# Split-half products for the attention values of every second chunk

## What is computed

```python
z = einsum('bqhd,bkhd->bhqk', q, k) * SB_SCALE + bias
mask = kpos[None, :] < qpos[:, None]
log_rest = where(mask, log_sigmoid(-z), 0.0)
after = cumsum(log_rest, axis=3, reverse=True) - log_rest
a = where(mask, exp(log_sigmoid(z) + after), 0.0)
out = einsum('bhqk,bkhd->bqhd', a, v)
```

## Time and profile before

| | |
|---|---|
| median of three runs | 1857.78 us |
| the profiled execution | 1855.77 us, its span 1854.0 us |
| granted TensorE clock, mean | 0.999 |
| busy over the span | PE 98%, PEld 93%, DVE 47%, ACT 28%, POOL 14% |
| the four pairs | about 68 us to 425 us of the span |
| one pair's 24 chunks | from 70.2 us; the next k projection starts at 139.98 us |

### The profile page before, as it was taken

One profiled execution on the slowest core, in us unless ns is written; L12 is line 12 of the kernel. 1 busy time (PEld: TensorE's weight loads), 2 busy tenths in 40 slices (PEclk: granted clock), 3 DMA queues, 4 the chain that ended last, 5 costly groups with the idle time before them and its releaser, 6 DMA issues.

```text
span 1854.0 us, 28837 instructions
## 1 busy us (share of the span) xinstructions
PE 1809.1 (98%) x11113; PEld 1721.2 (93%) x11113; DVE 871.3 (47%) x1111; ACT 524.3 (28%) x838; POOL 263.5 (14%) x309
## 2 busy tenths in 40 slices
PE   6999999999999999999999999999999999999997
PEld 6878787879799899999999889999999999999996
DVE  5565657475334423232242575552145542455536
ACT  5575757481100100000022542221112210122224
POOL 1121212120133211111111000000100001000002
PEclk9999999999999999999999999999999999999999
DMA  5202020205411111111131131111111111111312
GB/s 168 69 24 68 23 68 23 68 13 180 131 46 40 36 49 51 57 34 40 51 137 58 35 122 49 45 45 46 45 46 45 44 50 42 51 51 44 131 30 97
DMA packets 162282, 113.73 MB, mean 61 GB/s; under 512 B 5389, under 2 KB 152213, under 8 KB 161947
## 3 DMA queue, kind: packets, MB, share of 16 engines
q1 hardware_dynamic: 161035, 108.34, 19.6%
q10 hardware_dynamic: 1200, 4.75, 0.7%
HBM read 95.86 MB, written 13.40 MB: 59 GB/s over the span
## 4 chain that ended last, share of the span: by engine, by line
PE 87%; ACT 5%; DVE 4%; issue 2%; DMA 0%; SPq 0%; DVEq 0%; ACTq 0%; POOL 0%; POOLq 0%
PE ps L1490 67%; PE ps L1500 9%; PE misc L1584 2%; ACT zl L739 1%; ACT zl L744 1%; PE misc L1476 1%; PE ps L1770 1%; PE ps L1828 1%; PE ps L1714 1%; PE ps L1568 1%; PE misc L1788 1%; PE ps L1476 1%; ACT zl L749 1%; PE ps L1569 1%; PE ps L1574 0%
## 5 line engine op out<-in xcount | busy, mean ns | idle before, releaser
L1490 PE MATMUL ps<-h_hi,w_lo 128*128 128x344 f32 x1896 | 404.4, 322 | 1.9 <-DVE up L1359 1.1
L1490 PE MATMUL ps<-h_lo,w_hi 128*128 128x344 f32 x1896 | 402.8, 321 | 0.0
L1490 PE MATMUL ps<-h_hi,w_hi 128*128 128x344 f32 x1896 | 400.7, 320 | 0.0
L1072 DVE TENSOR_TENSOR w_lo<-stage,w_hi 128x1024 fp32r<-128x1024 f32 x148 | 198.6, 1342 | 335.8 <-POOL w_hi L573 334.8
L573 POOL TENSOR_SCALAR w_hi<-stage 128x1024 fp32r<-128x1024 f32 x148 | 158.8, 1073 | 1301.5 <-PE ps L1490 1064.7
L1490 PEld LDWEIGHTS ps<-h_hi,w_lo 128*128 128x128 f32 x1896 | 319.5, 188 | 4.3 <-issue 1.4
L1490 PEld LDWEIGHTS ps<-h_lo,w_hi 128*128 128x128 f32 x1896 | 321.2, 189 | 0.0
L1490 PEld LDWEIGHTS ps<-h_hi,w_hi 128*128 128x128 f32 x1896 | 316.3, 188 | 0.0
L1500 PE MATMUL ps<-h_hi,w_lo 128*128 128x344 f32 x408 | 135.6, 332 | 0.6 <-DVE a_raw L1167 0.5
L1359 DVE TENSOR_TENSOR up<-ps,work 128x1032 f32<-128x1032 f32 x44 | 54.2, 1233 | 166.6 <-PE ps L1490 163.3
L1500 PE MATMUL ps<-h_lo,w_hi 128*128 128x344 f32 x408 | 130.9, 321 | 0.0
(11 more groups left out here) (273 smaller groups left out, 2545.7 us busy)
## 6 DMA issues: line engine op xcount, KB each, us to landing
stage<-in_w_in SPq DMA_DIRECT2D x48, 512.0 KB, 3.9
stage<-in_w_up SPq DMA_DIRECT2D x44, 512.0 KB, 3.7
stage<-in_w_down SPq DMA_DIRECT2D x16, 448.0 KB, 3.3
stage<-in_w_branch SPq DMA_DIRECT2D x24, 256.0 KB, 2.7
x_scratch<-trunk SPq DMA_DIRECT2D x1, 4128.0 KB, 12.3
x_back<-x_scratch SPq DMA_DIRECT2D x1, 4128.0 KB, 13.5
x_tok<-in_x_prompt SPq DMA_DIRECT2D x8, 512.0 KB, 8.0
kv_pg<-in_cache_k SPq DMA_DIRECT2D x16, 256.0 KB, 3.8
```

The costliest lines, as they stand in the source:

```text
L1072: V.tensor_tensor(w_lo[par][:, :, :], stage[par][:, :, :], w_hi[par][:, :, :].bitcast(F32), ALU.subtract).then_inc(w_lo_made, 1)
L1490: last = M(ps[par][:, c, :], w[par][:, k, :], x[:, c * CH:(c + 1) * CH], start=(k == 0 and s == 0), stop=(k == n - 1 and s == 2))
```

## The change

- In even chunks `values` stays as it is. In odd chunks it is three fp32r products: `v_lo` with `att_hi`, `v_hi` with `att_lo`, `v_hi` with `att_hi`.
- Once a pair POOL makes `v_hi` (1024 columns, after `v_tok`), and DVE at its step 1 makes `v_lo` (1024 columns).
- For each odd chunk k POOL makes `att_hi` (behind `s_hi(k + 2)` in its queue; there is one buffer, so it also waits for the values of chunk k - 2), and DVE makes `att_lo` in place of `att` at the end of its step k + 3. For chunks 21 and 23 this lies behind the last `s_lo` and ahead of the last `w_lo`.
- There are three `att` buffers, not four, and `k_f` and `v_f` now lie under `att_hi`, `att2` and `v_hi`.
- PE takes the values at even steps c: first those of chunk c - 4, then those of chunk c - 5, with one increment of `pv_done` behind both. Before, it took c - 5 and c - 4 at odd steps.

```diff
-        att = [sb(f"att{i}", [P, HALF], F32, s_att) for i in range(2)] + [k_f[:, 0:HALF], k_f[:, HALF:2 * HALF]]
+        att = [sb(f"att{i}", [P, HALF], F32, s_att) for i in range(2)] + [att2]
...
+                def att_hi_of(c):
+
+                    W = CHUNKS[c][3]
+                    pool.wait_ge(att_ready, p * NCK + (c + 1))
+                    pool.wait_ge(pv_done, p * NCK + (c - 1 + NATT))
+                    pool.sem_inc(hi_begun, 1)
+                    nc.gpsimd.tensor_scalar(att_hi[:, 0:W], att[c % NATT][:, 0:W], 1.0, 0.0,
+                                            ALU.mult, ALU.add).then_inc(ahi_made, 1)
+
+                pool.wait_ge(vtok_made, p + 1)
+                pool.sem_inc(hi_begun, 1)
+                nc.gpsimd.tensor_scalar(v_hi, v_tok[:, :, :], 1.0, 0.0, ALU.mult, ALU.add).then_inc(vh_made, 1)
...
+                    if c >= 3 and c % 2 == 1:
+                        att_hi_of(c - 2)
+                att_hi_of(NCK - 1)
...
+                def att_lo_of(c):
+
+                    W = CHUNKS[c][3]
+                    dve.wait_ge(ahi_made, p * (NCK // 2) + (c + 1) // 2)
+                    a = att[c % NATT][:, 0:W]
+                    V.tensor_tensor(att_lo[c % NATT][:, 0:W], a, att_hi[:, 0:W].bitcast(F32), ALU.subtract).then_inc(alo_made, 1)
...
+                    if c == 1:
+                        dve.wait_ge(stack_in, p * 64 + 64)
+                        dve.wait_ge(vh_made, p + 1)
+                        V.tensor_tensor(v_lo, v_tok[:, :, :], v_hi.bitcast(F32), ALU.subtract)
+                    if c >= 4 and c % 2 == 0:
+                        att_lo_of(c - 3)
                 sums_lo(NCK - 1)
+                att_lo_of(NCK - 3)
+                att_lo_of(NCK - 1)
                 split_lo(1, p * 4 + 5)
...
-                    pe.wait_ge(att_ready, p * NCK + (c + 1))
-                    M(misc[:, q0:q0 + W], v_tok[:, kb, :], att[c % NATT][:, 0:W], start=top, stop=last,
-                      skip_group_check=True).then_inc(pv_done, 1)
+                    out = misc[:, q0:q0 + W]
+                    if c % 2 == 0:
+                        pe.wait_ge(att_ready, p * NCK + (c + 1))
+                        t = M(out, v_tok[:, kb, :], att[c % NATT][:, 0:W], start=top, stop=last, skip_group_check=True)
+                    else:
+                        pe.wait_ge(alo_made, p * (NCK // 2) + (c + 1) // 2)
+                        lo = att_lo[c % NATT][:, 0:W]
+                        M(out, v_lo[:, kb, :], att_hi[:, 0:W], start=top, stop=False, skip_group_check=True)
+                        M(out, v_hi[:, kb, :], lo, start=False, stop=False, skip_group_check=True)
+                        t = M(out, v_hi[:, kb, :], att_hi[:, 0:W], start=False, stop=last, skip_group_check=True)
+                    return t
...
-                    if c % 2 == 1 and 0 <= c - LAG_VALUES - 1 < NCK:
-                        values(c - LAG_VALUES - 1)
-                        values(c - LAG_VALUES)
+                    if c % 2 == 0 and c >= LAG_VALUES:
+                        done = 0
+                        for chunk in (c - LAG_VALUES, c - LAG_VALUES - 1):
+                            if 0 <= chunk < NCK:
+                                pv, done = values(chunk), done + 1
+                        pv.then_inc(pv_done, done)
```

More of the change, by code:

```diff
@@ L198, in build @@
         s_pair.close()
+        s_split = ExitStack()
+        sb("keys_below", [P, 3 * T], F32, s_split)
+        v_lo_all = sb("v_lo", [P, T], F32R, s_split)
+        att2 = sb("att2", [P, HALF], F32, s_split)
+        att_hi = sb("att_hi", [P, T - HALF], F32R, s_split)
+        v_hi_all = sb("v_hi", [P, T], F32R, s_split)
+        v_hi, v_lo = (v[:, 0:TP].rearrange("p (a b) -> p a b", b=P) for v in (v_hi_all, v_lo_all))
+        s_split.close()
+        s_low = ExitStack()
+        sb("split_below", [P, 4 * T], F32, s_low)
+        att_lo2 = sb("att_lo2", [P, HALF], F32R, s_low)
+        s_low.close()
         s_dec = ExitStack()
@@ L233, in build @@
         s_att.close()
+        s_low = ExitStack()
+        sb("att_below", [P, 14 * HALF], F32, s_low)
+        att_lo = [sb(f"att_lo{i}", [P, HALF], F32R, s_low) for i in range(2)] + [att_lo2]
+        s_low.close()
         spat = sb("spat", [P, SG, T], F32, s_mix)
@@ L326, in build @@
         (
-            params_in, gpre_in, consts, par_ps, par_sb, ss_made, std_made, rs_made, xn_made, xt_ps,
+            vh_made, ahi_made, alo_made, params_in, gpre_in, consts, par_ps, par_sb, ss_made, std_made, rs_made, xn_made, xt_ps,
             h_hi_made, w_hi_made, w_lo_made, unit_done, biasp_made, q_hi_made, kf_made, k_hi_made,
@@ L341, in build @@
         ) = (sem(n) for n in (
-            "params_in", "gpre_in", "consts", "par_ps", "par_sb", "ss_made", "std_made", "rs_made",
+            "vh_made", "ahi_made", "alo_made", "params_in", "gpre_in", "consts", "par_ps", "par_sb", "ss_made", "std_made", "rs_made",
             "xn_made", "xt_ps", "h_hi_made", "w_hi_made", "w_lo_made", "unit_done", "biasp_made",
```

## The result

The changed kernel takes 1869.36 us (median of 6 runs, 1868.17 to 1870.52), the one before, beside it, 1858.39 (6 runs, 1853.86 to 1860.72). The ratio is 1.0063, with a 95% interval of 1.0053 to 1.0073: 11.0 us slower, 9.8 to 13.6. The prediction was 1866.2 in a range of 1853 to 1875. Its sign and mechanism hold; the size is the top end of what it gave for its likeliest case (+8.4, 5 to 11). Of its three chances the largest (0.55) had gone to "the same", and 0.63% lies just past that bound, in the 0.39.

A forecast was written before the change was run, and what follows sets the result against it. Within a pair ACT bounds wide chunks, PE the narrow stretches and the tail. Three terms gave 1.25 to 2.7 us a pair, taken as 2.1: +8.4 on 1855.77 is 1864.2, as a median 1866.2 (range 1853 to 1875).

The forecast's parts named there:

- its likeliest case: The prediction's own forecast: four pairs add 8.4 us (5 to 11), 1862 to 1871; chance 50%.
- the same: Outcome not told from no change, about 0.5% or 9.3 us: between 1848.5 and 1867.1; chance 0.55.
- the 0.39: Chance of slower, above 1867.1: 0.24 from the forecast's own case and 0.15 from DVE's lag feeding back.
- The bound: In a pair, ACT where chunks are wide; cheaper matmuls count where ACT waits for PE (1.40, 1.15 us) and in the tail.
- First narrow stretch: Around chunks 8 to 11: ACT's wait for chunk 10 comes back one chunk later, plus 0.8 to 1.8 us a pair.
- Second narrow stretch: Chunks 20 to 23: same order, PE's chain from weights 16 reaches 123.1 against 122.89; plus 0.15 to 0.6 us a pair.
- The tail: End of a pair: values 20 ahead of the q projection start it 0.75 us later, what follows is shorter; net 0.3.
- The cover of the last `w_lo`: End of a pair: `w_lo` done at 139.6, PE needs it at 140.7, so 1.1 us of cover are left.
- The sum: Per pair 1.25 to 2.7 us, taken as 2.1 by half of the port waits; four pairs +8.4 us (5 to 11).
- DVE's lag feeds back all along: Rival: port waits make wide steps DVE's, plus 4 to 5 us per pair, 16 to 20 in all, 1876; chance 15%.
- The lag is absorbed: Rival: port waits near none, only the new order costs, 0.3 to 0.6 us per pair, 1856 to 1861; chance 25%.
- Faster: Rival: ACT's waits for PE go and don't come back, at most 2.55 us per pair, 1848, likelier 1852; chance 10%.

The follow-up runs named there:

- e11: The changed kernel without `att_hi`, `att_lo` and `v_lo`: new order and three fp32r products, `v_hi` kept; 1864.43 us, ratio 1.0038.
- e10: The changed kernel without `att_hi` and `att_lo`; `v_hi`, `v_lo`, the order and three fp32r products stay; 1865.63 us, ratio 1.0044.
- e2: The changed kernel without `att_lo`, the second product taking `att_hi` in its place; 1867.82 us, ratio 1.0058.
- e1: The kernel before with the new order of values (even steps, chunk c - 4 first), all native products, no halves; 1866.61 us, ratio 1.0052.
- the ladder: Pair periods: before 95.02; order alone 98.08; with fp32r products 96.85; with `v_lo` 97.35; with `att_hi` 97.75; with `att_lo` 98.19 us.
- e4: The kernel before with the values of one chunk (c - 5) at every step, all native; 1858.37 us, ratio 1.0007.
- e8: The kernel before with the two values of an odd step moved behind the scores of the next step, all native; 1858.34 us, ratio 1.0006.
- e6: The kernel before with values at even steps but the older chunk (c - 5) still first, all native; 1862.12 us, ratio 1.0024.
- e5: The kernel before's order (odd steps, c - 5 then c - 4) with halves made for even chunks, odd ones native; 1865.68 us, ratio 1.0049.
- e7: The changed kernel with the two values of an even step moved behind the next step's scores; 1880.24 us, ratio 1.0124.
- e12: As e7, with the last `w_lo` of a pair put ahead of `att_lo(21)` and `att_lo(23)` on DVE; 1876.63 us, ratio 1.0107.

## Why the prediction was right, and where its terms were off

Three of the signs that it gave for itself did not come: `s_lo(7)` was later than its 0.3 to 1.3 us, a pair took 3.17 longer and not 1.3 to 2.7, and PE's busy time did not fall. The two waits of ACT, the clock in the pairs and the three products 0.24 apart came as said.

**The bound.** It said that extra time counts in the narrow stretches, where ACT waits for PE, and in the tail. The wide steps, from chunk 11 to chunk 20, took 0.13 us less than before, the two narrow stretches 2.90 more, the tail 0.43. Right.

**First narrow stretch (0.8 to 1.8 forecast, 1.4 in the sum).** It took 1.87 in the second pair, and 2.31 in the first (97.85 - 69.42 against 94.35 - 68.23). The mechanism was right, waits vanished before chunk 10 and came back before 11. Its lower bound, with no lateness of DVE, was 0.8; e11, which has next to none, shows 26.90 - 26.03 = 0.87. Its chain from the end of `s_lo(7)` to chunk 11 was summed to 3.74 and took 97.85 - 93.87 = 3.98. What was under-sized is the lateness: `s_lo(7)` came 1.54 later, forecast 0.3 to 1.3. POOL's instructions held `sums` and `att_lo` too, which had been left out of the sum: `sums` beside `v_hi` took 0.80, and its group's mean rose from 346 ns before to 373 with `v_hi` alone (e10), 394 with `att_hi` (e2) and 416 in the changed kernel. The Trainium skill (GPSIMD Engine Reference, section 8, Key points) says that GpSimd contends with VectorE's instructions of two SBUF inputs; these rows agree, for `sums` as well.

**Second narrow stretch (0.15 to 0.6 forecast, took 1.03).** This is the term that failed most. Without lateness (e11) it is already (56.03 - 26.90) - (54.60 - 26.03) = 0.56 from chunk 11 to 23, and 0.69 from chunk 20 on ((56.03 - 48.27) - (54.60 - 47.53)). The chain from weights 16 to chunk 23 had been summed to 123.1 - 115.94 = 7.16; e11, with the same cheap products and next to no work added on DVE, took from the end of weights 16 to chunk 23 125.92 - 118.26 = 7.66. PE in the changed kernel shows what was short:

```profile
118.35 0.51 PE L1615 MATMUL ps<-s_lo,neg_tri 128*128 128x512 f32 x1 [0.76 <-DVE s_lo L1160]
...
119.86 1.02 PE L1633 MATMUL misc<-att,v_tok 128*128 128x512 f32 x2
...
121.64 0.23 PE L1607 MATMUL ps<-mask_b,ident_b 128*128 128x128 bf16 x1
121.68 0.48 PE L1615 MATMUL ps<-s_lo,neg_tri 128*128 128x512 f32 x1
122.00 0.40 PE L1616 MATMUL ps<-s_hi,neg_tri 128*128 128x512 f32 x1
122.23 0.40 PE L1619 MATMUL ps<-s_lo,neg_rest 128*128 128x512 f32 x1
122.47 0.40 PE L1621 MATMUL ps<-s_hi,neg_rest 128*128 128x512 f32 x1
```

Weights 16 were ready at 118.65 + 0.67 = 119.32, and PE took their values at 119.86, 0.54 later: it had stood 0.76 us before `softplus_sums(17)` for `s_lo`, so the chain began later than the sum had it. And the first running-sum product behind a mask holds PE for 0.32, not 0.23: a group of four is 1.02, not 0.92, and there are two. The last entry, from the start of `scores(23)` at 126.63 to ACT's start, took 0.74, not 0.56. From 119.86 to chunk 23's 127.37 it is 7.51, where the sum had 7.18. The forecast had allowed DVE a slip of 0.4 before it counts there; the row at 118.35 shows that PE already waited for it.

**The tail (0.3 forecast, took 0.43).** Right in size. e1 shows why: with native products its tail is 0.83 longer than before's, and with the cheap ones (e11, 74.85 - 56.03 = 18.82) 0.42. (Both are read to the `q_dec` copy, behind the last values. The first row of the next k projection starts 0.84 later than before's, but before's ran beside the end of a native product, by the prediction's 0.43.) The missing fourth `att` buffer cost nothing, as said: ACT's weights waited 8 times over the four pairs, each time for a running sum at the end of a pair, never for values. The cover of the last `w_lo` held, as said: it was done at 142.44 + 1.22 = 143.66, and the next k projection, which needs it, started 1.6 us later (forecast 1.1):

```profile
141.83 0.69 DVE L1177 TENSOR_TENSOR att_lo<-att,att_hi 128x512 fp32r<-128x512 f32 x1 [7.14 <-POOL att_hi L635]
142.44 1.22 DVE L1104 TENSOR_TENSOR w_lo<-stage,w_hi 128x1024 fp32r<-128x1024 f32 x1
```

```profile
145.28 0.64 PE L1537 MATMUL ps<-h_hi,w_lo 128*128 128x344 f32 x3
```

**The sum.** 1.25 to 2.7 a pair was forecast, 3.17 came in the trace. It splits as the ladder does: without lateness the forecast had 0.8 + 0.15 + 0.3 = 1.25 and e11 shows 1.83; for lateness it took 0.85 and the halves cost 1.34. The total came out nearer, and that is in part luck: the profiled execution of the kernel before lay 2.6 us under the median of its six runs, that of the changed kernel 0.1 under its own. Between the profiled executions the difference is 13.5, where 8.4 was forecast; between the medians it is 11.0. The clock ahead of the pairs, which differs from run to run, goes with such shifts, but no run here takes it out.

**The rivals.** *DVE's lag feeds back all along*: no, the wide steps show no growth, though DVE's waits in them have nearly gone (its `zl` waited 30.4 us for ACT over the four pairs before, 5.0 after). *The lag is absorbed*: no; between e11 and the changed kernel lie 1.34 us a pair. Its other half, 0.3 to 0.6 a pair for the order with cheap products and no lateness, is the case of e11, 1.83. *Faster*: no, and e4 and e8 show why. With native products, e4 leaves one value and e8 none ahead of any `scores`, and both are level with the kernel before. ACT's waits of 1.40 and 1.15 are not caused by the place of the values alone.

**What stays open.** Why the younger chunk first costs e1 0.7 us a pair outside the tail as well: in the second pair 0.16 of it is there by chunk 11, 0.37 by chunk 20 and 0.73 by chunk 23, but no run took only this part away. PE also waits for weights just made at chunks 8 and 12 there (0.16 and 0.57 us in the second pair), which e6 does not, so these waits are the likely cause. The granted clock: rows show it fall to 0.50 after stops of PE in e5, e7 and e12, and without any stop ahead of the pairs, and no run says when it does and when it does not. And e4's +0.47 a pair: its time can't be told from before's.

## What to carry to other kernels

A cheaper product on one engine is bought with work and waits on others: add up when each half is ready and who stands behind the wait, not only busy time. When a change moves work between steps to make room for a new producer, run the new order alone with the old arithmetic: here it was nearly the whole loss, and the saving of the products was paid for by making their halves. On in-order engines it matters which of two tasks of one step comes first: taking the one whose operand is younger made PE wait where the other could have run. And before a wait of one kernel is compared with another's, look at the granted clock of that window: the longest wait in e5 lay in a fall of it.

## What the runs showed of the hardware that was not expected

An instruction of POOL on SBUF and one of DVE with two inputs in SBUF held each other not only where it was seen before: `sums` 0.35 became 0.80 beside `v_hi`, `s_lo` 0.69 became 1.00 beside `att_hi`, `att_lo` 0.68 became 0.88 beside an `s_hi` of 0.52 and, in e7, 1.53 beside a `w_hi` of 1.05. POOL's own instructions stretched too (`att_hi` 0.62 to 1.07 at 93.28 us, behind the `s_lo` at 92.41 and beside `sums`). In these rows DVE's loss was never more than the POOL instruction's own length, and DVE's `zl`, which reads PSUM, kept its 0.74 beside an `s_hi` (86.56 us). And PE's busy time is a poor measure of what a product costs: with the same order the native ones gave 1814.3 us (e1), the split ones 1808.9 (e11), 5.4 less, where the distances of starts say 6.7; but e1 and the kernel before, with the same products, differ as much (1814.3 and 1809.1). A stop of PE can cost more than its own length: after three of the stops of 2.44 us in e7 and e12 the granted clock stood at 0.50 for about 3 us, and the pair took another 1.3 to 1.5 us.
